# Two buffers of normed rows before the expert blocks, the second block's rows turned later, and the tenth expert matrix loaded after the token table

## The chip, the cores and the metric

The kernel runs on one core of a Trainium2 chip. The metric is device time in microseconds (us) of one execution; lower is better. TensorE is called PE, VectorE DVE, ScalarE ACT, GpSimd POOL and SyncE SP. SP and POOL mostly issue DMAs here.

## The reference, cut to what matters

One layer of a hybrid encoder on 512 prompt frames and 32 sample frames (544 tokens, width 1024): a token mixer (attention and a gated delta net, joined by an output projection) and then a mixture of 32 experts. Everything is in float32. The part that this change touches is the join of the two:

```python
x1 = x + einsum('btd,de->bte', gate_a * branch_a + gate_b * branch_b, w_out)
n = rmsnorm(x1, g_ffn)
grp_logits = n @ w_grp + b_grp           # 4 groups: pick the best
e_logits   = n @ w_exp + b_exp           # 32 experts: the best 2 inside that group
# each expert e, for the tokens that chose it:
h = silu(n[tok] @ w_e1[e]) * (n[tok] @ w_e3[e])
y[tok] += (h @ w_e2[e]) * weight
```

Each expert has three matrices of 2 MB (w_e1 and w_e3 1024x512, w_e2 512x1024); all 32 experts are read, 96 matrices in all.

## The kernel before, in words

The last part of the kernel is written in two functions whose engine programs run one behind the other on each engine: `project_and_choose`, then `expert_blocks`. The order of the work is written out by hand, and semaphores join the engines.

`project_and_choose` goes through five tiles of token rows (four of 128 prompt rows, i = 0 to 3, then the 32 sample rows, i = 4). For each tile PE finishes the second half of the output projection (L2084, counted in `projected`), DVE adds it to the residual rows (L2435), ACT forms the sum of squares and its root (L2287, L2288), DVE the reciprocal (L2439, `inverted`). PE turns the rows (L2313), ACT moves them out of the bank to `xT` (L2268), PE multiplies them with the router's weights (L2324), and DVE picks group and experts (L2442 to L2460) and counts ranks (L2420, L2424).

Beside it each tile's rows are written to a table in DRAM, `token_rows`, from which the expert blocks later gather. ACT scales the rows into one buffer `c_xn` (L2296) and POOL issues the DMA of 512 KB to the table (L2256). As there is one buffer, ACT waits ahead of L2296 until the table write of the tile before has landed (`tabled`, the wait at L2293). Everything that stands behind on ACT waits too: the move of the next tile's turned rows (L2268) first. The sample rows have two buffers of their own (L2300, L2259, `last_tabled`).

SP issues the expert matrices, each a DMA of 2 MB on one queue, in the order w_e1, w_e3, w_e2 of experts 0, 1 and 2, then w_e1 and w_e3 of expert 3 (eleven matrices, of which the tenth is w_e1 of expert 3, in buffer `e_w1_3`). The first six have no wait. The seventh waits for `projected` 2, the eighth for `projected` 4, the ninth and the tenth for `projected` 5, the eleventh (buffer `e_w3_3`, in which many small tiles of this function lie) for `normed` 5 and `picked`, the list of slots that DVE makes last (L2476).

`expert_blocks` runs 32 blocks, one for each expert (64 slots each), and further ones where an expert has more tokens. The first block's rows are picked on PE (L2350). Of the others POOL gathers the rows from the table (L2751 for blocks 1 and 2 once `last_tabled` is complete, L2541 later). A block on PE: up products with w_e1 and w_e3 (L2593, 64 matmuls), then the rows of the next block are turned (`ahead`, L2562 to L2566), then the hidden rows are turned (L2602), then the down product (L2611, 16 matmuls). Each buffer of weights is loaded again once its product is over: there are four for w_e1 and w_e3 and three for w_e2, and for the first of the reloads (L2183) w_e1 and w_e3 go in halves. Behind the last block the results, scattered to DRAM by choice, are read back and added (`y_rows`).

Of the kernel before, what the change touches and what calls it, by code (L numbers as in the profile page):

```python
# [19 lines left out]
ACT = mybir.ActivationFunctionType  # L20
AX = mybir.AxisListType

D = 1024
KD = D // 128
# [2079 lines left out]
ROW0 = [NP] + [128 * t for t in range(4)]  # L2104
# [63 lines left out]
def load_weights(k, sp, name, tiles, loaded, e, slot):  # L2168

    src = expert_matrix(k, name, e).rearrange("(p k) n -> p (k n)", p=128)  # L2170
    sp.dma_start(tiles[slot][:].rearrange("p k n -> p (k n)"), src).then_inc(loaded[slot], 16)  # L2171
# [20 lines left out]
def load_down(k, sp, e, slot):  # L2192

    src = expert_matrix(k, "w_e2", e).rearrange("(a p b) n -> p a (b n)", a=2, p=128)
    sp.dma_start(k.w2[slot][:].rearrange("p (a b) n -> p a (b n)", a=2), src).then_inc(k.w2_loaded[slot], 16)


def project_and_choose(k):
# [3 lines left out]

    nc, o = k.nc, k.out_stream
    V, T = nc.vector, k.early
    xn, xn_s, junk, xT = k.xn, k.xn_s, k.xn_s[1], [T(f"xT{m}", 4, 128) for m in range(3)]
    s0, s1, rt, rr = T("sum0", 5), T("sum1", 5), T("root", 5), T("rms", 5)
    iN, sN, token_i = T("iota_i", NE, dt=I32), T("slot_i", 2 * SLOTS, dt=I32), T("token_i", 5, dt=I32)
    gi, gf, pen, em, ei, ef = T("gidx", 8, dt=U32), T("gsel", 1), T("penalty", GROUPS), T("em", NE), T("eidx", 8, dt=U32), T("esel", 2)
    both, run, tmp = T("both", 3, NE), T("run", 2, NE), T("tmp", NE)
    r1, b1 = [T(f"rank_oh{j}", 2 * SLOTS) for j in range(2)], T("blk_oh", 2, NE)  # L2210
    made, padded, zeroed, based, weighed, added0, added1, squared, rms, tabled, turned, moved, scored, biased, chosen, \
        counted, ranked, listed, projected, columns, inverted, k.picked, k.normed = (k.sem("c_" + n) for n in (
            "made", "padded", "zeroed", "based", "weighed", "added0", "added1", "squared", "rms", "tabled", "turned", "moved",
            "scored", "biased", "chosen", "counted", "ranked", "listed", "projected", "columns", "inverted", "picked", "normed"))
    sums = both[:, 0:2, :].rearrange("p a e -> p (a e)")
    other, scaled = T("first_other", SLOTS), T("first_scaled", 1)
    k.tabled, placed = tabled, k.sem("c_placed")
    P, TA, TB, L, C, S = k.bank[0:2], k.bank[2], k.bank[3], k.bank[4:6], k.bank[6], k.bank[7]
    slot = lambda i: i % 2 if i < 4 else 2
    tiles = [(i, t, TILES[t][0], TILES[t][1]) for i, t in enumerate(ORDER)]  # L2220
    def on_sync(sp):
        for j in (2 * KD - 2, 2 * KD - 1):
            o.load(sp, j)
        sp.wait_ge(padded, 2)
        load_router(k, sp)
        for e in range(2):
            load_up(k, sp, e, e)
            load_down(k, sp, e, e)
        sp.wait_ge(projected, 2)
        load_weights(k, sp, "w_e1", k.w1, k.w1_loaded, 2, 2)  # L2230
        sp.wait_ge(projected, 4)
        load_weights(k, sp, "w_e3", k.w3, k.w3_loaded, 2, 2)
        sp.wait_ge(projected, 5)
        load_down(k, sp, 2, 2)
        load_weights(k, sp, "w_e1", k.w1, k.w1_loaded, 3, 3)
        sp.wait_ge(k.normed, 5)
        sp.wait_ge(k.picked, 1)
        load_weights(k, sp, "w_e3", k.w3, k.w3_loaded, 3, 3)

    def on_gpsimd(g):  # L2240
        g.memset(k.wr[:], 0.0).then_inc(padded, 1)
        g.memset(k.br[:], NEG).then_inc(padded, 1)
        g.iota(iN[:], pattern=[[1, NE]], base=0, channel_multiplier=0).then_inc(made, 1)

        g.iota(sN[:].rearrange("p (a g r) -> p a g r", a=2, r=SPREAD), pattern=[[0, 2], [1, SLOTS // SPREAD], [SLOTS // SPREAD, SPREAD]],
               base=0, channel_multiplier=0).then_inc(made, 1)

        g.iota(token_i[:], pattern=[[256, 5]], base=-256 - 2 * NT, channel_multiplier=2).then_inc(made, 1)
        g.wait_ge(made, 3)
        g.iota(token_i[:, 0:1], pattern=[[0, 1]], base=2 * NP - 2 * NT, channel_multiplier=2).then_inc(made, 1)  # L2250
        for j in (2 * KD - 2, 2 * KD - 1):
            o.split_lo(g, j)
        for i, t, c0, n in tiles:
            g.wait_ge(k.normed, i + 1)
            if i < 4:
                g.dma_start(k.table[ROW0[t]:ROW0[t] + n, :], xn[0:n, :]).then_inc(tabled, 16)  # L2256
            else:
                for h in range(2):
                    g.dma_start(k.table[ROW0[t]:ROW0[t] + n, 512 * h:512 * h + 512], xn_s[h][0:n, :]).then_inc(k.last_tabled, 16)  # L2259
        g.wait_ge(tabled, 64)  # L2260

    def on_scalar(a):
        def move(i, n, h, bank):
            m = 2 * i + h
            a.wait_ge(turned, m + 1)
            if m >= 3:
                a.wait_ge(scored, m - 2)
            nc.scalar.activation(xT[m % 3][:, :, 0:n], bank[:, 0:4 * n].rearrange("p (k n) -> p k n", k=4), ACT.Copy)\  # L2268
                .then_inc(moved, 1)

        c = k.chain(a, "scalar")
        for j in (2 * KD - 2, 2 * KD - 1):
            o.split_hi(a, j)
        a.wait_ge(zeroed, 1)
        for i, t, c0, n in tiles:
            a.wait_ge(added0, i + 1)
            nc.scalar.activation(junk[0:n, :], k.x[0:n, t, 0:512], ACT.Square, accum_out=s0[0:n, t:t + 1]).then_inc(squared, 1)
            a.wait_ge(squared, i + 1)
        move(0, tiles[0][3], 0, TA)
        for s in range(1, RING):  # L2280
            nc.scalar.activation(k.xg[:, s, :], k.striu[:, 0:1].broadcast_to([128, D // 2]), ACT.Copy).then_inc(k.cleared, 1)
        a.wait_ge(based, 1)
        for i, t, c0, n in tiles:
            if i >= 1:
                move(i, n, 0, TA)
            a.wait_ge(added1, i + 1)
            c(nc.scalar.activation(junk[0:n, :], k.x[0:n, t, 512:], ACT.Square, accum_out=s1[0:n, t:t + 1]))  # L2287
            nc.scalar.activation(rt[0:n, t:t + 1], s1[0:n, t:t + 1], ACT.Sqrt, bias=s0[0:n, t:t + 1],  # L2288
                                 scale=1.0 / D).then_inc(rms, 1)
            move(i, n, 1, TB)  # L2290
            a.wait_ge(inverted, i + 1)
            if 1 <= i < 4:
                a.wait_ge(tabled, 16 * i)  # L2293
            rows = k.x[0:n, t, :].rearrange("n (p k) -> n p k", k=KD)
            if i < 4:
                nc.scalar.activation(xn[0:n, :].rearrange("n (k p) -> n p k", k=KD), rows, ACT.Copy,  # L2296
                                     scale=rr[0:n, t:t + 1]).then_inc(k.normed, 1)
            else:
                for h in range(2):
                    last = nc.scalar.activation(xn_s[h][0:n, :].rearrange("n (k p) -> n p k", k=4), rows[:, :, 4 * h:4 * h + 4],  # L2300
                                                ACT.Copy, scale=rr[0:n, t:t + 1])
                last.then_inc(k.normed, 1)
# [179 lines left out]
def expert_blocks(k):  # L2482
# [4 lines left out]
    nc = k.nc  # L2487
# [8 lines left out]
    xT, hm, hT = k.xT, k.hm, k.hT  # L2496
    y = k.over("b_y", [128, D // 2], F32, "late", 16 * KD * FE)
    T = lambda name, *dims: k.sb("m_" + name, [128] + list(dims), F32, ctx)
# [19 lines left out]
    turned, copied = k.turned, k.copied  # L2518
# [140 lines left out]
    def places(b):  # L2659

        up_at = (b, 0) if b <= RING else ((b - 1) % RING, (b - 1) // RING)
        return up_at + (b % RING, b // RING, b % RING, b // RING - (b % RING == 0))

    def run_blocks(eng, part, beside=lambda s: None):

        for b in range(EARLY):
            part(eng, b, *places(b), False, places(b + 1)[4:])
            beside(b)
        eng.wait_ge(planned, 1)
        n = eng.value_load(k.nmore[0:1, 0:1], min_val=0, max_val=MORE)  # L2670
        with eng.Fori(EARLY // RING, LAST // RING - 1) as i:
            for s in range(RING):
                d2, past_d2 = (s + 1) % RING, (s + 1) // RING
                after = (s + 2) % RING
                part(eng, RING * i + s + 1, s, i, d2, i + past_d2, d2, i + past_d2 - (d2 == 0), False,
                     (after, i + (s + 2) // RING - (after == 0)))
        for b in range(LAST - RING + 1, NE - 1):
            part(eng, b, *places(b), False, places(b + 1)[4:] if b < LAST else None)
            beside(b)
        u, nu, d2, nd, half, m = places(LAST)  # L2680
        with eng.If(n > 0):
            with eng.Fori(0, n) as j:
                part(eng, j + NE - 1, u, j + nu + 1, d2, j + nd + 1, half, j + m + 1, True)
        part(eng, n + NE - 1, *places(NE - 1), True, halves=True)
        return n
# [159 lines left out]
    def on_vector(v):  # L2845
# [88 lines left out]
        c(V.tensor_copy(which[:], S[:, 0:2 * NE]))  # L2934
        c(V.tensor_tensor(which[:], which[:], S[:, 2 * NE:4 * NE], ALU.add))
        aim(which, NE, k.dst[:, 0:NE]).then_inc(targets, 1)
        v.wait_ge(k.tabled, 64)
        run_blocks(v, vector_part, beside)
        def add_choice(m, j, before):
            t = ORDER[m]  # L2940
# [87 lines left out]
```

## Time and profile before

| | |
|---|---|
| median of 3 runs | 1210.57 us (1208.8 to 1213.7) |
| time of the profiled execution | 1210.81 us |
| its span | 1209.1 us |
| PE busy | 1083.7 us (90%) |
| DVE, ACT, POOL busy | 36%, 29%, 32% |
| DMA over the span | 284.52 MB, mean 235 GB/s |
| mean granted clock of TensorE | 0.974 |
| largest share of the chain that ended last | 20%, DMA of expert weights |

The span is what the trace covers, 1.7 us less than the execution's own time. The granted clock is a share of 2.4 GHz: 1.00 is that level, 0.50 is 1.2 GHz. A DMA share is the mean busy share of the core's 16 DMA engines, and a share slightly above 1 is a full one. All times inside the trace are counted from the start of the span.

### The profile page before, as it was taken

The numbers are of one execution on the slowest core, as the hardware profiler recorded it, in microseconds if no ns is written. First come the engines' busy times: TensorE is split into PE (matmuls) and PEld (weight loads), VectorE is DVE, ScalarE is ACT, GpSimd is POOL, SyncE is SP. The second block draws the span as 40 slices with busy tenths as digits, with TensorE's granted clock in tenths as the row PEclk, the third lists the DMA queues.
The fourth block names the chain that finished last, engine by engine and source line by source line (L and its number), as shares of the span: only waits on it lengthen the run. The fifth ranks groups of instructions, "written<-read, shape, count | busy, mean of one in ns | idle before, by whom it ended". The sixth has DMA issues, their size and how long they took to land. (4 is left out here: it accounts for less than half of the span.)

```text
span 1209.1 us, 20612 instructions
## 1 busy us (share of the span) xinstructions
PE 1083.7 (90%) x8278; PEld 833.0 (69%) x8278; DVE 434.3 (36%) x995; ACT 355.1 (29%) x752; POOL 388.2 (32%) x426
## 2 busy tenths in 40 slices
PE   5999899899999989999999988999998777777777
PEld 4998888799999877888899764555554444444443
DVE  6598733793111264432242453222111111111115
ACT  5547633452222644453333422000000000000000
POOL 3554359843211443232464201212212111111100
PEclk9999989998988989999999988999999999999999
DMA  6422225345332621112531598999999999999998
GB/s 131 88 70 71 71 66 160 88 131 146 89 91 58 203 102 53 53 41 82 188 96 53 201 428 348 419 424 427 426 427 429 428 428 428 427 428 429 428 423 332
DMA packets 149677, 284.52 MB, mean 235 GB/s; under 512 B 43636, under 2 KB 118996, under 8 KB 132704
## 3 DMA queue, kind: packets, MB, share of 16 engines
q1 hardware_dynamic: 94288, 244.94, 52.0%
q10 hardware_dynamic: 49632, 27.46, 8.1%
q0 software_dynamic: 5680, 11.05, 2.4%
q8 instruction: 54, 0.88, 0.3%
q14 instruction: 23, 0.19, 0.0%
HBM read 266.81 MB, written 24.31 MB: 241 GB/s over the span
## 5 line engine op out<-in xcount | busy, mean ns | idle before, releaser
L2593 PE MATMUL bank<-e_w,b_xT 128*64 128x256 f32 x2048 | 231.3, 381 | 42.4 <-DMA e_w<-in_w_e 40.1
L499 PE MATMUL bank<-xhi,cv_w_hi 128*128 128x272 f32 x848 | 258.8, 305 | 8.6 <-PEq L145 2.6
L485 POOL TENSOR_TENSOR cv_w_lo<-cv_w_raw,cv_w_hi 128x1024 fp32r<-128x1024 f32 (+1 forms) x69 | 165.7, 2402 | 311.8 <-ACT cv_w_hi L478 311.4
L499 PE MATMUL bank<-xhi,cv_w_lo 128*128 128x272 f32 x848 | 249.5, 294 | 0.0
L499 PE MATMUL bank<-xlo,cv_w_hi 128*128 128x272 f32 x848 | 248.9, 294 | 0.0
L2593 PEld LDWEIGHTS bank<-e_w,b_xT 128*64 128x64 f32 x2048 | 149.1, 137 | 133.1 <-DMA e_w<-in_w_e 36.3
L499 PEld LDWEIGHTS bank<-xhi,cv_w_hi 128*128 128x128 f32 x848 | 164.4, 194 | 17.3 <-issue 9.7
L499 PEld LDWEIGHTS bank<-xlo,cv_w_hi 128*128 128x128 f32 x848 | 164.8, 194 | 1.0
L499 PEld LDWEIGHTS bank<-xhi,cv_w_lo 128*128 128x128 f32 x848 | 164.2, 194 | 0.0
L2638 DVE TENSOR_TENSOR b_hidden<-b_hidden,bank 128x256 f32<-128x256 f32 x32 | 13.5, 421 | 364.4 <-PE bank L2593 364.4
L2611 PE MATMUL bank<-e_w,b_hiddenT 128*64 128x512 f32 x512 | 116.9, 598 | 22.3 <-DVE b_hiddenT L2643 22.3
L2621 ACT ACTIVATE b_y<-bank 128x512 f32<-128x512 f32 x32 | 19.1, 597 | 299.2 <-PE bank L2611 299.2
L2550 POOL COPY b_target<-slot_target 128x1 int32 (+1 forms) x31 | 5.5, 177 | 312.3 <-ACT b_y L2621 280.2
L2611 PEld LDWEIGHTS bank<-e_w,b_hiddenT 128*64 128x64 f32 x512 | 37.2, 136 | 80.0 <-issue 52.0
L478 ACT ACTIVATE cv_w_hi<-cv_w_raw 128x1024 fp32r<-128x1024 f32 (+1 forms) x69 | 69.3, 1004 | 27.7 <-DMA cv_w_raw<-in_w_br_a 15.8
L687 DVE SCALAR_TENSOR_TENSOR conv_acc<-conv_in,wconv,conv_acc 128x547 f32<-128x547 f32 x48 | 60.5, 1260 | 1.7
L2618 ACT ACTIVATE b_hidden<-bank 128x256 f32<-128x256 f32 x32 | 12.3, 383 | 115.8 <-PE bank L2593 115.8
L2084 PE MATMUL bank<-o_hi,mix_prompt 128*128 128x512 f32 x128 | 43.2, 397 | 1.4 <-PEq L145 0.7
L499 PE MATMUL bank<-yb_hi,cv_w_hi 128*128 128x272 f32 x128 | 41.5, 324 | 1.4 <-DVE yb_lo L1657 1.4
L499 PE MATMUL bank<-yb_lo,cv_w_hi 128*128 128x272 f32 x128 | 38.4, 300 | 0.0
L499 PE MATMUL bank<-yb_hi,cv_w_lo 128*128 128x272 f32 x128 | 38.3, 299 | 0.0
L1926 ACT ACTIVATE f_probs<-f_probs,f_stat 32x160 f32<-32x160 f32 (+4 forms) x40 | 21.1, 528 | 54.8 <-DVE f_stat L1873 54.7
(449 smaller groups left out, 1660.4 us busy)
## 6 DMA issues: line engine op xcount, KB each, us to landing
e_w<-in_w_e SPq DMA_DIRECT2D x91, 2048.0 KB, 37.4
cv_w_raw<-in_w_in ACTq DMA_DIRECT2D x34, 512.0 KB, 3.9
e_w<-in_w_e SPq DMA_DIRECT2D x10, 1024.0 KB, 33.3
cv_w_raw<-in_w_in SPq DMA_DIRECT2D x18, 512.0 KB, 3.7
cv_w_raw<-in_w_br_b ACTq DMA_DIRECT2D x8, 512.0 KB, 4.0
o_raw<-in_w_out SPq DMA_DIRECT2D x16, 256.0 KB, 3.7
y_rows<-choice_rows SPq DMA_DIRECT2D x8, 512.0 KB, 7.0
g_values_gates<-g_z_stage ACTq DMA_DIRECT2D x12, 272.0 KB, 4.3
```

Of the source, the lines that this page charges most:

```text
L478: self.k.nc.scalar.activation(self.whi[:, c % OPS, 0:nk, :], self.raw[:, c % RAWS, 0:nk, :], ACT.Copy)\
L485: self.k.nc.gpsimd.tensor_tensor(self.wlo[:, s, 0:nk, :], self.raw[:, s, 0:nk, :], self.whi[:, c % OPS, 0:nk, :].bitcast(F32), ALU.subtract)\
L499: last = self.k.nc.tensor.matmul(self.bank(c, h)[:, 0:HALF], w, x[:, d, cols], start=(d == 0 and n == 0), stop=(d == nk - 1 and n == 2))
L687: op = nc.vector.scalar_tensor_tensor(out=ac[:, 0:W], in0=ci[:, w:w + W], scalar=k.wconv[:, w, c:c + 1], in1=ac[:, 0:W], op0=ALU.mult, op1 ...
L1926: last = nc.scalar.activation(pr[0:n, j % 2, x, 0:nk], pr[0:n, j % 2, x, 0:nk], ACT.Exp, bias=st[0:n, 1, 2 * j + x:2 * j + x + 1], accum_o ...
L2084: last = k.nc.tensor.matmul(bank[0:n, :], rows, w[:, d, :], start=(start and i == 0), stop=(d == KD - 1 and i == 2))
L2550: nc.gpsimd.tensor_copy(to[:], k.dst[:, bass.ds(column, 1)]).then_inc(aimed, 1)
L2593: last = nc.tensor.matmul(k.bank[bank][sl[a], 0:FH], xT[:, d, :], w[u][:, d, FH * a:FH * a + FH], start=(d == 0), stop=(d == KD - 1))
L2611: last = nc.tensor.matmul(k.bank[4][sl[a], :], hT[:, f % 2, sl[f // 2]], k.w2[d2][:, f, 512 * a:512 * a + 512], start=(f == 0), stop=(f == ...
L2618: nc.scalar.activation(hm[:], k.bank[1][:, 0:FH], ACT.Silu).then_inc(silu, 1)
L2621: nc.scalar.activation(y[:], k.bank[4][:], ACT.Copy).then_inc(out, 1)
L2638: nc.vector.tensor_tensor(hm[:], hm[:], k.bank[2][:, 0:FH], ALU.mult).then_inc(hidden, 1)
```

## The change

The normed rows get a second buffer, `xn_odd`, which lies among the small tiles in `e_w3_3`; tiles 0 and 2 use the old one, tiles 1 and 3 the new one. Each buffer has its own semaphore `tabled[j]`. ACT's wait ahead of L2296 now stands for tiles 2 and 3 alone, for the table write of two tiles before. On SP the tenth matrix is issued behind two waits, for `normed` 5 and for `last_tabled` 32, so once the sample rows' table writes have landed; the eleventh also waits for the second buffer's two table writes. In the expert blocks, block 0 no longer turns block 1's rows between its up and down products; block 1 turns them itself at its beginning, behind block 0's down product (`own` is true for b == 1).

```diff
-    xn, xn_s, junk, xT = k.xn, k.xn_s, k.xn_s[1], [T(f"xT{m}", 4, 128) for m in range(3)]
+    xn, xn_s, junk, xT = [k.xn, T("xn_odd", D)], k.xn_s, k.xn_s[1], [T(f"xT{m}", 4, 128) for m in range(3)]
...
-    k.tabled, placed = tabled, k.sem("c_placed")
+    k.tabled = tabled = [k.sem(f"c_tabled{j}") for j in range(2)]
+    placed = k.sem("c_placed")
...
         sp.wait_ge(projected, 5)
         load_down(k, sp, 2, 2)
+        sp.wait_ge(k.normed, 5)
+        sp.wait_ge(k.last_tabled, 32)
         load_weights(k, sp, "w_e1", k.w1, k.w1_loaded, 3, 3)
-        sp.wait_ge(k.normed, 5)
         sp.wait_ge(k.picked, 1)
+        sp.wait_ge(tabled[1], 32)
         load_weights(k, sp, "w_e3", k.w3, k.w3_loaded, 3, 3)
...
             if i < 4:
-                g.dma_start(k.table[ROW0[t]:ROW0[t] + n, :], xn[0:n, :]).then_inc(tabled, 16)
+                g.dma_start(k.table[ROW0[t]:ROW0[t] + n, :], xn[i % 2][0:n, :]).then_inc(tabled[i % 2], 16)
...
-        g.wait_ge(tabled, 64)
+        for j in range(2):
+            g.wait_ge(tabled[j], 32)
...
-            if 1 <= i < 4:
-                a.wait_ge(tabled, 16 * i)
+            if 2 <= i < 4:
+                a.wait_ge(tabled[i % 2], 16)
             rows = k.x[0:n, t, :].rearrange("n (p k) -> n p k", k=KD)
             if i < 4:
-                nc.scalar.activation(xn[0:n, :].rearrange("n (k p) -> n p k", k=KD), rows, ACT.Copy,
+                nc.scalar.activation(xn[i % 2][0:n, :].rearrange("n (k p) -> n p k", k=KD), rows, ACT.Copy,
                                      scale=rr[0:n, t:t + 1]).then_inc(k.normed, 1)
...
         for b in range(EARLY):
-            part(eng, b, *places(b), False, places(b + 1)[4:])
+            part(eng, b, *places(b), b == 1, places(b + 1)[4:] if b else None)
             beside(b)
...
-        v.wait_ge(k.tabled, 64)
+        for j in range(2):
+            v.wait_ge(k.tabled[j], 32)
```

## Rows read from the trace of the kernel before

**Rows 1.** The page's slices of the span in 40 parts: DMA busy share and rate.

```profile
DMA  6422225345332621112531598999999999999998
GB/s 131 88 70 71 71 66 160 88 131 146 89 91 58 203 102 53 53 41 82 188 96 53 201 428 348 419 424 427 426 427 429 428 428 428 427 428 429 428 423 332
```

**Rows 2.** Busy time by stretch: length, PE, PEld, DVE, ACT, POOL, clock, DMA share, GB/s.

```profile
683.00:725.00 42.00, 39.05 (x216) 31.07 (x215) 20.64 (x109) 16.36 (x26) 1.91 (x3) 0.92 1.01 422
725.00:728.00 3.00, 0.00 (x0) 0.00 (x0) 1.34 (x9) 1.83 (x2) 0.00 (x0) 0.69 0.77 303
728.00:738.00 10.00, 9.29 (x46) 4.70 (x46) 4.72 (x29) 3.46 (x8) 1.56 (x3) 0.58 1.02 390
738.00:743.00 5.00, 4.24 (x54) 2.61 (x54) 2.69 (x11) 0.73 (x1) 1.13 (x1) 1.00 0.46 127
743.00:760.00 17.00, 15.22 (x129) 8.84 (x127) 3.67 (x14) 3.52 (x7) 5.04 (x10) 1.00 1.00 404
760.00:893.00 133.00, 125.40 (x977) 69.92 (x975) 26.68 (x78) 9.81 (x20) 29.43 (x62) 1.00 1.01 426
893.00:1169.00 276.00, 220.37 (x1676) 123.97 (x1672) 33.31 (x88) 18.62 (x38) 50.57 (x108) 1.00 1.01 428
```

**Rows 3.** The chain that ended last, in order of time: start, length, what.

```profile
689.57 10.77 DMA token_rows<-c_xn
...
714.77 11.31 DMA token_rows<-c_xn
...
732.77 7.93 DMA token_rows<-c_xn_sample
...
741.61 8.49 DMA b_rows<-token_rows,slot_token
...
897.34 35.60 DMA e_w<-in_w_e
```

**Rows 4.** Timeline of ACT, 700 to 730: start, length, line, idle before and its releaser.

```profile
704.64 0.60 ACT L2268 ACTIVATE c_xT<-bank 128x512 f32<-128x512 f32 x1 [0.70 <-PE bank L2313]
712.44 2.04 ACT L2296 ACTIVATE c_xn<-x_rows,c_rms 128x1024 f32<-128x1024 f32 x1 [7.21 <-DMA token_rows<-c_xn]
...
714.28 0.62 ACT L2268 ACTIVATE c_xT<-bank 128x512 f32<-128x512 f32 x1
...
726.17 2.02 ACT L2296 ACTIVATE c_xn<-x_rows,c_rms 128x1024 f32<-128x1024 f32 x1 [8.56 <-DMA token_rows<-c_xn]
```

**Rows 5.** Timeline of PE, 706 to 751.

```profile
706.20 0.48 PE L2084 MATMUL bank<-o_hi,mix_prompt 128*128 128x512 f32 x1
...
714.96 1.12 PE L2324 MATMUL bank<-c_w_router,c_xT 128*128 128x40 f32 x8 [2.20 <-ACT c_xT L2268]
...
719.38 0.63 PE L2084 MATMUL bank<-o_hi,mix_sample 128*32 128x512 f32 x1
...
728.35 0.74 PE L2324 MATMUL bank<-c_w_router,c_xT 128*32 128x40 f32 x8 [3.57 <-ACT c_xT L2268]
...
741.75 7.13 PE L2593 MATMUL bank<-e_w,b_xT 128*64 128x256 f32 x64 [0.53 <-DVE b_xT L2629]
750.14 0.32 PE L2562 MATMUL bank<-ident,b_rows 64*128 64x64 f32 x1 [1.26 <-DMA b_rows<-token_rows,slot_token]
```

**Rows 6.** SP's queue, the issues of weights from 709 to 749.

```profile
709.22 0.33 SPq L2171 DMA_DIRECT2D e_w<-in_w_e  x1
723.88 0.38 SPq L2195 DMA_DIRECT2D e_w<-in_w_e  x1
...
740.53 0.33 SPq L2171 DMA_DIRECT2D e_w<-in_w_e  x1
743.74 5.51 SPq L2183 DMA_DIRECT2D e_w<-in_w_e  x4
```

**Rows 7.** The table writes of the four prompt tiles (L2256), issue to landing.

```profile
DMA to landing us min/median/max: 9.5/11.0/11.9
```

**Rows 8.** The page's DMA issues: count, KB each, median us from issue to landing.

```profile
out_y_p<-x_rows SPq DMA_DIRECT2D x4, 512.0 KB, 3.3
```

More of the change, by code:

```diff
@@ L2210, in project_and_choose @@
     r1, b1 = [T(f"rank_oh{j}", 2 * SLOTS) for j in range(2)], T("blk_oh", 2, NE)
-    made, padded, zeroed, based, weighed, added0, added1, squared, rms, tabled, turned, moved, scored, biased, chosen, \
+    made, padded, zeroed, based, weighed, added0, added1, squared, rms, turned, moved, scored, biased, chosen, \
         counted, ranked, listed, projected, columns, inverted, k.picked, k.normed = (k.sem("c_" + n) for n in (
-            "made", "padded", "zeroed", "based", "weighed", "added0", "added1", "squared", "rms", "tabled", "turned", "moved",
+            "made", "padded", "zeroed", "based", "weighed", "added0", "added1", "squared", "rms", "turned", "moved",
             "scored", "biased", "chosen", "counted", "ranked", "listed", "projected", "columns", "inverted", "picked", "normed"))
```

## The prediction

> **What bounds the kernel now.** I read the page's slices first [rows 1]: up to slice 22 the DMA engines are half idle, and from slice 23 (about 695 us) to the end they are full, at 419 to 429 GB/s but for slice 24 with 348. That is the reading of expert weights, and slice 24 (725 to 756 us) is where this change works. Then the stretches [rows 2]. From 743 us to 1169 us, 426 us long, the DMA share is 1.00 to 1.01 at 404 to 428 GB/s. PE is busy 94% of 760 to 893 and only 80% of 893 to 1169 (220.37 of 276). Third the chain of waits [rows 3]. Before 742 us it runs over ACT's normed rows and the table writes (10.77, 11.31 and 7.93 us stand in the rows, a fourth of 9.47 us lies between, 39 us in sum), then over a gather and PE's blocks, and from 897 us on it is made of hops on the weights, 35.6 us and longer. The chain would have one gain from everything that goes off the first part. But PE's early lead is given back: whatever PE gains before 893 it waits for afterwards, because the weights' stream through the DMA engines is full from 743 us on. So the question is when that stream could have been at the same place, that is, how much time the DMA engines idle between 683 and 743 us, and not when PE starts its blocks.
>
> That idle time, length times one less the share [rows 2]: 725 to 728, 3 x 0.23 = 0.7 us; 738 to 743, 5 x 0.54 = 2.7 us. Together 3.4 us. The rate is also lower where table writes are mixed in: 728 to 738 at 390 instead of 428 GB/s is 10 x 38/428 = 0.9 us, 743 to 760 at 404 is 1.0 us, 683 to 725 at 422 is 0.6 us. Even all of it recovered makes 5.9 us, 0.5% of the time; nothing here can give more unless the reason above is wrong.
>
> **The change part by part.**
>
> *ACT's wait for the table.* It removes waits of 4.8 us (tile 1, not in the rows), 7.21 us and 8.56 us ahead of L2296 [rows 4]. Tile 1's hides behind PE: PE's later chunk of projection starts at 706.20 after a gap of 0.3 us or so in either case, so I count nothing. For tile 2 ACT is free at 705.24 [rows 4] and the first table write landed at 700.34 [rows 3], so the normed rows are made from 705.3 to 707.3. The turned rows of tile 3, which ACT moved at 714.28 only because it stood in that wait [rows 4], are moved as soon as PE has turned them, and PE doesn't idle the 2.20 us before 714.96 [rows 5]. Its router product starts at about 712.7. From there to the next chunk of projection it took 4.42 us (714.96 to 719.38), in the preceding tile about 3.15 us at clock 1.00; the chunk itself took 719.38 to 723.88 [rows 5, 6], 4.5 us, against 706.20 to 709.22, 3.0 us. The clock between was 0.50 for most of that (mean 0.92 over 683 to 725 [rows 2]), that is the 1.2 GHz level, and it fell just behind the idle 2.20 us. I take it that it doesn't fall: `projected` 5 comes at 712.7 + 3.15 + 2.9 = 718.8 instead of 723.9. If it falls all the same, 712.7 + 4.4 + 4.5 = 721.6. For tile 3 the wait goes too (the second write lands near 709). The 3.57 us of idle PE before 728.35 [rows 5] go with it; the router product of the sample rows starts at about 720, 8 us earlier, and the sample's normed rows, made at 729.9 to 732.0 before, at about 721.5 to 723.5. Late next is DVE's choice, about 3 us a tile, and PE's first rows. From the sample's router product to the first block it was 728.35 to 741.75, 13.4 us, at mean clock 0.58 over most of it; at clock 1.00 some 2 us less. So block 0 starts at 720 + 11.5 = 731.5 with the clock up, and at about 735 with it down: 7 to 10 us earlier.
>
> *The table.* The five tiles' writes are issued at 689.6, 698, 707.5, 717.3 and 723.5/724. Under the full stream they took 9.5 to 11.9 us each [rows 7], the sample's 7.93 us [rows 3]. Two of them are now under way at once for the first time, so nothing in this trace prices that. From below: no dearer, the last lands at 724.0 + 7.9 = 731.9. From above: strictly one behind the other, 689.6 + 10.8 + 9.5 + 11.3 + 11.9 + 7.9 = 741. I take 732, since before too the queue of weights beside each write was full, and 512 KB in 11 us is a ninth of the rate, which leaves room for a second.
>
> *The tenth matrix behind the table.* The ninth is issued at `projected` 5, at 719 (721.6 at worst). The eighth, issued at 709.22 [rows 6], ran the engines dry only at 725, so the dip of 0.7 us is gone. Without the tenth the engines run dry at 738.7 (where the share falls in 738 to 743) less one matrix, 2.1 MB at 428 GB/s = 4.9 us, less the 0.7: at 733.1. The tenth is issued at the landing, 732, and its first bytes come 0.7 us behind (the eleventh, issued at 740.53 [rows 6], had the engines busy again at about 741.2): 732.7. That is a hair ahead of the dry point, but the landing of a write comes after its last byte, and each start of the queue before had a ramp of about half a us. I take a gap of 0.8 us; bounds nothing (landing at 731 or earlier) and 8.6 us (landing at 741). The eleventh waits for `picked`, 10 us earlier like block 0, so at 731 to 734, and the tenth covers until 738. The reloads (L2183) start at 733 to 737 instead of 743.74, with two matrices, 9.8 us, queued ahead of them. No further gap.
>
> *The Trainium skill against this step.* Before, the engines ran dry at about 738.7 and the gathers behind `last_tabled` were issued at 741.61 [rows 3], some 2 us behind the last byte. "DMA: Bandwidth & Descriptors", section "Anatomy of one DMA", gives about 2 us of fixed cost, most of it the receipt of the write, heaviest for HBM. By it a load that waits for a table write can't follow on without a gap: if the table is the last in the queue the gap is about 2 us and 0.7 us for the start, and the gain 0.7 us instead of 2.6 us. The trace agrees with the size; whether the table is last here it doesn't tell. Both results lie in the range.
>
> *The second block's rows.* In block 0 PE's wait of 1.26 us for the gather goes [rows 5], and the turn, 0.6 us, moves. In block 1 the turn and DVE's two scaled copies of 0.42 us stand alone: +1.5 us of PE. The gather, 8.49 us [rows 3], lands at about 741, ahead of block 0's end at 731.5 + 12.4 = 744. PE net -1.3 to +1.8 us; on the end nothing, as PE's lead of several us over the stream up to 893 hides it. Were this cover gone it would cost +0.2 us.
>
> *Semaphores and the second buffer.* Two waits on POOL and DVE in place of one, a few tens of ns each, off the path: nothing. The buffer's overlap with `e_w3_3` only matters by the added wait, met by then (731.9).
>
> **The sum.** Gap before 3.4 us, gap after 0.8 us: -2.6 us, against the profiled execution 1210.81 - 2.6 = 1208.2. That execution lies 0.2 us above the median of the runs (1210.57), so the median becomes 1208.0; with the rate beside the table unchanged I leave 1208.2.
>
> **The rivals.**
>
> A. *The gap stays.* The table's landing or the clock takes away what the earlier projection brings: landing at 734.5, gap 734.5 + 0.7 - 733.1 plus a ramp of 0.5 = 2.6 us, or the tenth matrix's new wait leaves the engines as idle as before. Gain 0 to 0.8 us, time 1210.3. For it: the receipt; that the tenth is queued later relative to the table than it was. Against: the 5 us by which the projection ends earlier.
>
> B. *PE's start sets the end.* Block 0 starts 7 to 10 us earlier and the end follows: 1210.6 - 8.5 = 1202. For it: the chain of waits runs over PE until 893. Against: DMA share 1.01 over 133 us of it, and PE's idle 20% behind it [rows 2]. I can think of no way but a rate above 428 GB/s.
>
> C. *Slower: the writes hold each other up.* Place: the sample rows' table write. If two writes in flight share one write's pace, the last lands at up to 741; the tenth matrix, the eleventh and all reloads stand behind it on SP, and the engines are dry from 733.1 to 741.7, 8.6 us against 3.4: +5.2 us, 1215.8. It costs from a landing at 735.5 on. For it: the 11 us under load. Against: with the weights gone the writes have the engines alone, and 512 KB out of SBUF took 3.3 us outside this full stream [rows 8]. So the likelier size is a landing at 735 to 736, and the 741 an end.
>
> D. *The change doesn't do what it says*: PE or DVE is late where ACT was, and `projected` 5 comes at 723 anyway. Then the tenth matrix issues 8 us later than before (at the old landing, 740.8), the engines are dry from 733.8 to 741.5, and the time is 1210.6 + 5 = 1215.5. Against: each of the waits on ACT is put down to the table's write.
>
> **How the numbers follow.** The forecast (gap of 0 to 2 us, 1206.8 to 1209.5) has 0.60, A 0.20, C 0.08, D 0.05, B 0.07. The predicted time is the forecast's, 1208.2. Runs of before spread by 5 us, so a median can be off by 1.5 us. The range 1204.8 to 1212.0 holds the forecast and A with that spread (0.8 less the spread's tails, and the milder part of C); outside lie B, D and most of C. What a measurement of this kernel can tell from no change is about 0.5%, 6 us: faster means below 1204.5, which is B and a tail, 0.09; slower means above 1216.6, which only the ends of C and D with the spread reach, 0.06; same 0.85.
>
> **What would show it.** In the trace after: no idle ahead of L2296 for tile 1, and little for 2 and 3; PE's 2.20 and 3.57 us gone; clock 1.00 from 716 to 723 (else the second value holds); ninth matrix issued near 719; sample's table landed at 732, tenth issued behind it at once; DMA share in a stretch around 733 with a single dip of under 1.5 us; block 0 at 731 to 735; PE waiting for weights already from about 860 instead of 893; and from 745 on the same 424 to 428 GB/s. The forecast is wrong if the stream after the dip is not full, if the landing comes after 735, or if the end moves by more than the idle DMA time does.

## The result

The changed kernel took 1204.83 us (median of 12 runs), the kernel before 1211.72 us: ratio 0.9947, 95% interval 0.9924 to 0.997, that is 0.3 to 0.8% faster and 6.4 us by the ratio. One of the 12 runs of the kernel before took 4914 us and can't belong to this ratio; without it the median is 1210.57 us. Another 12 runs of the changed kernel (e5 below) gave a median of 1207.89 us and a ratio of 0.9959 (0.9938 to 0.998). The forecast, 1208.2 us and so 2.6 us less, had the direction and the place right and about half the size. The time lies 0.03 us above the lower end of the stated range, 1204.8. That it lies inside is luck, as the median of the same kernel differs by 3 us between the two sets of runs; it is also only 0.3 us short of the 1204.5 from which the forecast would have called it faster, with a chance of 0.09.

The page of the changed kernel has the DMA engines full from slice 23 on. Slice 24, with 348 GB/s before [rows 1], has 422:

```profile
DMA  6422225445332531112632499999999999999998
GB/s 132 89 71 71 71 66 158 91 117 147 97 97 57 184 123 54 50 40 67 201 92 67 167 423 422 427 427 425 425 428 429 427 428 428 428 428 429 429 422 323
```

The same stretches as in [rows 2], of the changed kernel (columns as there: length, PE, PEld, DVE, ACT, POOL, clock, DMA share, GB/s):

```profile
683.00:725.00 42.00, 40.48 (x248) 31.11 (x246) 24.59 (x133) 22.53 (x34) 3.48 (x6) 0.96 1.01 423
725.00:728.00 3.00, 3.00 (x18) 1.11 (x16) 1.56 (x10) 0.00 (x0) 0.00 (x0) 0.96 0.95 401
728.00:738.00 10.00, 9.24 (x102) 6.03 (x102) 2.98 (x12) 3.27 (x5) 3.59 (x5) 1.00 1.02 429
738.00:743.00 5.00, 3.86 (x22) 1.48 (x20) 2.64 (x10) 0.00 (x0) 0.00 (x0) 1.00 0.99 416
743.00:760.00 17.00, 15.86 (x132) 8.91 (x130) 4.40 (x18) 1.58 (x3) 3.96 (x9) 1.00 1.02 424
760.00:893.00 133.00, 125.33 (x987) 70.53 (x985) 24.65 (x66) 10.22 (x21) 30.93 (x65) 1.00 1.01 427
893.00:1169.00 276.00, 216.19 (x1631) 121.29 (x1629) 32.55 (x86) 17.70 (x36) 47.91 (x102) 1.00 1.01 427
```

The two dry places, shares 0.77 and 0.46 [rows 2], are 0.95 and 0.99 now: of 3.4 us idle DMA time, counted by the share, 0.2 us is left. The rates beside them went up too, from 390 to 429 and from 404 to 424 GB/s.

ACT, start and length, with the idle time before and its releaser; to be read against [rows 4]:

```profile
704.98 2.10 ACT L2300 ACTIVATE c_xn<-x_rows,c_rms 128x1024 f32<-128x1024 f32 x1
709.54 0.60 ACT L2272 ACTIVATE c_xT<-bank 128x512 f32<-128x512 f32 x1 [2.46 <-PE bank L2317]
...
714.51 2.10 ACT L2300 ACTIVATE c_xn_odd<-x_rows,c_rms 128x1024 f32<-128x1024 f32 x1
...
721.51 2.14 ACT L2304 ACTIVATE c_xn_sample<-x_rows,c_rms 32x512 f32<-32x512 f32 x2 [0.67 <-DVE c_rms L2443]
```

No copy of normed rows waits for a table write; ACT now waits for PE and DVE. PE, against [rows 5]:

```profile
714.67 1.08 PE L2328 MATMUL bank<-c_w_router,c_xT 128*128 128x40 f32 x8 [0.32 <-ACT c_xT L2272]
715.59 0.41 PE L2084 MATMUL bank<-o_hi,mix_sample 128*32 128x512 f32 x1
...
719.38 0.47 PE L2328 MATMUL bank<-c_w_router,c_xT 128*32 128x40 f32 x8
...
731.49 7.13 PE L2597 MATMUL bank<-e_w,b_xT 128*64 128x256 f32 x64 [0.53 <-DVE b_xT L2633]
...
743.84 0.32 PE L2566 MATMUL bank<-ident,b_rows 64*128 64x64 f32 x1
...
745.04 7.13 PE L2597 MATMUL bank<-e_w,b_xT 128*64 128x256 f32 x64 [0.58 <-DVE b_xT L2633]
```

The idle 2.20 and 3.57 us are gone and block 0 starts at 731.49 instead of 741.75. SP's issues of weights, against [rows 6]:

```profile
718.56 0.38 SPq L2195 DMA_DIRECT2D e_w<-in_w_e  x1
729.69 1.08 SPq L2171 DMA_DIRECT2D e_w<-in_w_e  x2
733.48 5.51 SPq L2183 DMA_DIRECT2D e_w<-in_w_e  x4
```

The ninth matrix goes out 5.3 us earlier, the tenth and the eleventh together once the table is complete. The sample rows' two table writes, issued from 723.94 on, took 5 us each to land (the first line; in the kernel before, the chain has 7.93 us [rows 3]), the prompt tiles' 9.4 to 10.8 us (the second line), no more than before [rows 7]. They hardly overlap: they are issued at 689.67, 698.31, 707.37 and 716.90, so each is at most 2 us on its way when the one before lands:

```profile
DMA to landing us min/median/max: 4.9/5.0/5.1
...
DMA to landing us min/median/max: 9.4/10.1/10.8
```

The chain of waits up to 887 us runs over PE, with pieces on DVE and ACT between and without a DMA, and then over the weights. The last line is a matrix from its issue to its landing; the one that stands in this place before was issued 10 us later [rows 3]:

```profile
721.93 3.53 PE bank L2354 x8
...
731.49 7.15 PE bank L2597 x64
...
883.67 3.48 PE bank L2597 x32
...
887.31 40.56 DMA e_w<-in_w_e
```

So PE's blocks start 10.3 us earlier and the span is 5.5 us shorter (1203.6 against 1209.1): about half of what PE gained is waited off later. PE's first wait for a matrix ends at 897.24 in the changed kernel (the first line) and at 922.65 before (the second), and from 760 to 1170 us PE waits 43.1 us for weights instead of 40.1:

```profile
897.24 3.67 PE L2597 MATMUL bank<-e_w,b_xT 128*64 128x256 f32 x32 [1.39 <-DMA e_w<-in_w_e]
...
922.65 3.67 PE L2593 MATMUL bank<-e_w,b_xT 128*64 128x256 f32 x32 [1.06 <-DMA e_w<-in_w_e]
```

### The profile page after: what moved, and what is told of

The parts are those of the page before. It is cut to its first block and busy times, and to the rows that moved or that the text cites. A ratio compares the mean times of both kernels' runs of the same rounds, so it can differ in the third digit from the quotient of the medians.

```text
span 1203.6 us, 20613 instructions
## 1 busy us (share of the span) xinstructions
PE 1076.3 (89%) x8278; PEld 826.9 (69%) x8278; DVE 432.1 (36%) x995; ACT 356.6 (30%) x752; POOL 389.3 (32%) x426
## 5 line engine op out<-in xcount | busy, mean ns | idle before, releaser
L2597 PE MATMUL bank<-e_w,b_xT 128*64 128x256 f32 x2048 | 231.6, 381 | 46.1 <-DMA e_w<-in_w_e 43.1
## 6 DMA issues: line engine op xcount, KB each, us to landing
e_w<-in_w_e SPq DMA_DIRECT2D x10, 1024.0 KB, 33.3
```

The source lines that it names most:

```text
L2597: last = nc.tensor.matmul(k.bank[bank][sl[a], 0:FH], xT[:, d, :], w[u][:, d, FH * a:FH * a + FH], start=(d == 0), stop=(d == KD - 1))
```

## The experiments

Eight kernels, one of them the changed kernel again, were timed with 12 runs each against the kernel before. A second measure comes from the trace. The first expert matrix is issued at 676.5 to 685.0 us in executions of kernels that are the same up to there (e8, where that issue was moved, aside). That spread is as large as the runs' own, so the table gives the time from that issue to the end of the span as well. The last two columns are the bytes moved in 80 us, from 1 us behind that issue on (five stretches of 45, 3, 10, 5 and 17 us, length times rate), and the rate in 743:760 or the stretch that answers to it.

| kernel | ratio to before (95%) | first issue to end | MB in 80 us | GB/s then |
|---|---|---|---|---|
| before | | 529.1 us | 30.8 | 404 |
| after | 0.9947 (0.9924 to 0.997) | 523.6 | 33.5 | 425 |
| e5 after again | 0.9959 (0.9938 to 0.998) | 523.4 | 33.5 | 426 |
| e1 two buffers | 0.9953 (0.9931 to 0.9975) | 523.7 | 33.4 | 424 |
| e4 buffers, turn | 0.9953 (0.993 to 0.9977) | 523.9 | 33.3 | 423 |
| e2 tenth only | 1.0009 (0.9988 to 1.0031) | 530.8 | 30.6 | 394 |
| e3 turn only | 1.0011 (0.9987 to 1.0035) | 530.2 | 30.6 | 399 |
| e6 tenth late | 1.0009 (0.9986 to 1.0031) | 528.4 | 31.1 | 419 |
| e7 PE late | 0.9965 (0.9941 to 0.9988) | 523.7 | 33.5 | 425 |
| e8 stream early | 0.9956 (0.9932 to 0.9979) | 524.4 | 33.0 | 423 |

**e1, two buffers alone.** The changed kernel with its other two parts put back:

```diff
         load_down(k, sp, 2, 2)
-        sp.wait_ge(k.normed, 5)
-        sp.wait_ge(k.last_tabled, 32)
         load_weights(k, sp, "w_e1", k.w1, k.w1_loaded, 3, 3)
+        sp.wait_ge(k.normed, 5)
         sp.wait_ge(k.picked, 1)
...
-            part(eng, b, *places(b), b == 1, places(b + 1)[4:] if b else None)
+            part(eng, b, *places(b), False, places(b + 1)[4:])
```

> The change without its other two parts: two buffers of normed rows alone; the tenth matrix issued with the ninth as before, the second block's rows turned inside block 0 as before. Theory S (the end moves by the time that the weights' DMA engines are not full between 681 and 760 us, and by nothing else): the tenth matrix is queued at about 719, the queue covers until 738, the eleventh comes with `picked` at 730.5, so there is no dry stretch: all of the whole change's gain, 5 to 6 us, DMA share 0.97 or more in 725:743. Rival T (the earlier landed token table, got by holding the tenth matrix back, carries part of it): a gain of 3 us or less, the sample's table write landing 8 us after its issue instead of 5.7, and PE waiting about 1 us in block 0 for the gather.

All of the gain is there: 523.7 us. The stretches behind the first issue (at 684.98) have no dry place (columns: length, granted clock, DMA share, GB/s):

```profile
685.95:730.95 45.00, 0.96 1.01 412
730.95:733.95 3.00, 1.00 0.97 410
733.95:743.95 10.00, 1.00 1.03 432
743.95:748.95 5.00, 0.85 0.99 417
748.95:765.95 17.00, 0.94 1.02 424
```

Rival T falls on the end: PE does wait 1.94 us for the gather in block 0, as it said, and that doesn't reach the end. Its other sign didn't come: the sample's two table writes, issued from 729.95 on, took 4.9 and 5.5 us, against 4.9 and 5.1 in the changed kernel, and not 8. The first gather is issued 7.05 us behind the first of them here and 7.28 us there.

**e4, the whole change without the tenth matrix's move.**

```diff
-        sp.wait_ge(k.normed, 5)
-        sp.wait_ge(k.last_tabled, 32)
         load_weights(k, sp, "w_e1", k.w1, k.w1_loaded, 3, 3)
+        sp.wait_ge(k.normed, 5)
```

> The whole change but for the tenth matrix, which is issued with the ninth as before. Theory S: same as the whole change, as neither has a dry stretch (5 to 6 us less than before). Rival T: 1 us or more slower than the whole change.

523.9 us, 0.3 us from the whole change and as near to e1: nothing that this measure can tell.

**e2, the tenth matrix's move alone,** on the kernel before:

```diff
+        sp.wait_ge(k.normed, 5)
+        sp.wait_ge(k.last_tabled, 32)
         load_weights(k, sp, "w_e1", k.w1, k.w1_loaded, 3, 3)
-        sp.wait_ge(k.normed, 5)
```

> The kernel before with the tenth matrix alone moved behind the landed token table. Theory S: the engines run dry at about 733 instead of 738.7; the sample's table write, issued at 732.3, then has them to itself and lands near 736; the tenth follows, then the eleventh at 740.5; the dry time is 3 to 4 us instead of 3.4: no change, -0.5 to +2 us. Rival T: faster by 2 us or more, since the gathers start some 5 us earlier. Rival Q (a matrix less of cover is a matrix lost): slower by 4.9 us.

No change in time, 1.7 us more in the trace, inside theory S's bounds and against both rivals. The dry place moved to earlier stretches (first issue at 680.51):

```profile
726.48:729.48 3.00, 0.93 0.92 276
729.48:739.48 10.00, 0.68 0.83 283
739.48:744.48 5.00, 1.00 0.97 374
744.48:761.48 17.00, 0.90 0.99 394
```

But theory S's measure, the time that the engines are not full, doesn't give these 1.7 us. By the share 2.3 us are idle here, against 2.8 us in the same stretches of the kernel before (3 x 0.05 + 10 x 0.04 + 5 x 0.44), so the end should have come a little earlier. The bytes have the right sign: 0.26 MB less in the 80 us, 0.6 us at 428 GB/s, and 424 instead of 426 GB/s over the next 133 us, another 0.6 us. The remaining 0.5 us stay open.

**e3, the second block's turn alone,** on the kernel before:

```diff
-            part(eng, b, *places(b), False, places(b + 1)[4:])
+            part(eng, b, *places(b), b == 1, places(b + 1)[4:] if b else None)
```

> The kernel before with the second block's rows turned behind block 0's down product and nothing else. Theory S: PE's blocks move by -1.3 to +1.8 us, the weights' stream doesn't: no change, within 0.5 us in the trace from 681 us on. Rival P (where PE's blocks stand sets the end, as the chain of waits has it until 893 us): the end moves with block 1, by -1.3 to +1.8 us.

No change in time, 1.1 us more in the trace, over the 0.5 us of theory S. In this execution the clock was 0.51 in the ten us ahead of block 0 and the stream was dry for longer (first issue at 682.23):

```profile
731.20:741.20 10.00, 0.51 0.80 333
741.20:746.20 5.00, 0.82 0.46 108
746.20:763.20 17.00, 0.95 0.99 399
```

That is 10 x 0.20 + 5 x 0.54 = 4.7 us idle, against 2.8 in the same stretches of the kernel before. In bytes it is 0.29 MB less, 0.7 us, and 425 instead of 426 GB/s over the next 133 us is another 0.3, together 1.0 of the 1.1 us. The edit acts only behind the up products of block 0, which begins at 744.45, when most of the dry time is over, so most of this difference can't come from the edit. Block 1 also began 2.2 us later, and this run alone doesn't separate the two. e7 does.

**e6, the tenth matrix held back.** In the changed kernel:

```diff
         sp.wait_ge(k.last_tabled, 32)
+        sp.wait_ge(k.begun, 2)
         load_weights(k, sp, "w_e1", k.w1, k.w1_loaded, 3, 3)
```

> The changed kernel with the tenth matrix held back on purpose, until block 0's product with w_e3 is half done (about 5.3 us into block 0). PE's blocks start as in the changed kernel. Theory S (dry time of the stream sets the end, one for one): nine matrices and the table run out at about 732, the tenth's first bytes come at 737.6: some 5.5 us dry, so 5 to 6.5 us more from the first issue to the end, about 529. Rival P (PE's blocks set the end while they are the chain): no change, 523.6, since block 3, the first to need the tenth, is 35 us away.

4.9 us more than the changed kernel's two executions (523.5 on average), and the gain is gone in the timed runs too (1.0009). PE's block 0 starts 51.2 us behind the first issue as before this edit (51.0 and 51.5), block 1 at 64.7 (64.6 and 65.0); only the stream is interrupted:

```profile
724.37:727.37 3.00, 1.00 0.96 403
727.37:737.37 10.00, 1.00 0.64 208
737.37:742.37 5.00, 1.00 0.96 405
742.37:759.37 17.00, 1.00 1.00 419
```

Idle are 3.9 us by the share. In bytes it is 2.4 MB less in the 80 us than in the changed kernel, 5.7 us at 428 GB/s, so the 4.9 us lie between the two measures, and just under theory S's 5 to 6.5. Rival P falls.

**e7, PE held back.** In the changed kernel, ahead of block 0, with six more matmuls in float32 into a bank that is written again:

```diff
         pe.wait_ge(k.joined, 1)
+        pe.wait_ge(k.w1_loaded[0], 16)
+        for d in range(6):
+            nc.tensor.matmul(k.bank[1][:], k.ident[:], k.w1[0][:, d, :], start=True, stop=True)
         turn_first().then_inc(turned, 1)
```

> The changed kernel with six more matmuls of 128x512 in float32 on PE ahead of block 0, into a bank that is written again later: by the rows of this kernel about 0.85 us each, 5.1 us. Theory S: no change from the first issue to the end (523.6 within 0.5 us), since the two matrices queued behind the table cover the later reloads and PE only waits less from 880 us on. Rival P: 5 us more.

The extra work took 5.42 us and block 0 started at 740.63 - 684.26 = 56.4 us behind the first issue, 4.9 and 5.4 us later than in the changed kernel's two executions:

```profile
733.23:743.23 10.00, 1.00 1.02 433
743.23:748.23 5.00, 1.00 0.98 412
748.23:765.23 17.00, 1.00 1.02 425
```

The stream went on full and the end came at 523.7 us; PE waited 39.3 us for weights from 760 to 1170 instead of 43.1. PE's place can move by 5 us without a trace at the end: this and e6 together show that the stream sets the end and PE's blocks don't.

**e8, the stream started earlier.** In the changed kernel the first matrix goes out behind three of the six router DMAs, and DVE waits for the other three later:

```diff
         load_router(k, sp)
-        for e in range(2):
-            load_up(k, sp, e, e)
-            load_down(k, sp, e, e)
+        load_weights(k, sp, "w_e1", k.w1, k.w1_loaded, 0, 0)
+        load_router(k, sp, True)
+        load_weights(k, sp, "w_e3", k.w3, k.w3_loaded, 0, 0)
+        load_down(k, sp, 0, 0)
+        load_up(k, sp, 1, 1)
+        load_down(k, sp, 1, 1)
```

> The changed kernel with the first expert matrix issued ahead of the last three of the six small router DMAs (the biases and the gain, which now have a semaphore of their own that DVE waits for at the first tile's logits). The first matrix is issued about 1.6 us earlier in the stage, and all behind it. Theory S: the end comes 1 to 1.6 us earlier, counted from the first router DMA; against the kernel before 7 us. Rival P: the same or later, since the biases land behind 2 MB and DVE can be late with the first tile by a few us, which moves PE's blocks later by as much.

Counted from the first router DMA it took 527.4 us, the changed kernel's two executions 527.8 and 527.9. A gain of 0.4 to 0.5 us instead of 1 to 1.6, so theory S's number missed, and in the timed runs none that can be told (0.9956 beside 0.9959). The first matrix went out 1.1 and 1.5 us earlier than in those two, but the second to the sixth 0.1 to 0.8 us later, as three small DMAs stood between, and the stream ran at 403 GB/s in its first 45 us instead of 415:

```profile
675.42:720.42 45.00, 0.96 0.99 403
```

No version of these is clearly better than the changed kernel.

**e5, the changed kernel again,** with no edit.

> The changed kernel once more, on the chip of the next three. From the issue of the first expert matrix to the end of the span it took 523.6 us, the kernel before 529.1; the part ahead of that issue has differed by 8.5 us between executions of programs that are alike there (676.5 to 685.0), so the span alone is a poor measure. Both theories: 523.6 within 0.5 us.

523.4 us: the measure repeats within 0.2 us where the times themselves spread by 8 us.

## Why the prediction was right in its reason and short in its size

**The bound.** Right. The end moves with the weights' stream and not with PE (e6, e7). Over all ten executions the bytes in the 80 us go with the end: from the kernel before to the changed one 2.6 MB more is 5.5 us less, where 2.6 MB at 428 GB/s would be 6.2 us.

**ACT's wait and PE's times.** Right: `projected` 5 at 718.8 forecast, the ninth matrix issued at 718.56; sample rows issued at 723.5/724, measured 723.94 and 0.5 us later. Block 0 at 731.5, measured 731.49, is in part luck: the sample rows' router product began at 719.38 instead of 720, and from there it took 12.1 us instead of 11.5. The granted clock, 0.50 behind the idle 2.20 us before, stayed at 1.00 from 716 to 721. It was 0.50, the 1.2 GHz level, from 722 to 725, behind an idle 0.68 us and a stretch of small router matmuls, in the first rows' products, which took 3.53 us for 8 matmuls where the next 12 took 2.90 us. By these two PE paid some 1.6 us for it, an estimate; e7 shows that the end paid nothing.

**The gap before.** The first term that was mis-sized: 3.4 us, counted as length times one less the DMA share. A share is time, and the stream is bytes. In 738 to 743 the share was 0.46 but the rate only 127 GB/s, 0.30 of the full 428. By the rate the two dry places [rows 2] are 3 x 125/428 = 0.9 and 5 x 301/428 = 3.5 us, 4.4 us in all, 1.0 us more than forecast. With it the bound for everything recovered is 6.9 us and not 5.9.

**The gap after.** The second: 0.8 us, with a landing at 732. The table had landed by 729.69, as the sample's writes took 5 us, not 7.9, and the engines were not dry by then. What is left is 0.2 us by the share and 0.3 us by the rate (3 x 27/428 + 5 x 12/428), 0.5 us of the miss. That "nothing in this trace prices" two writes at once was a misreading: before, tile 3's write (issued at 728.48, 11.9 us on its way) and the sample's (from 732.25 on, 7.2 and 7.9 us) were under way together for 8 us, and in the changed kernel they overlap by 3.4 us only.

The sentence from the Trainium skill, "DMA: Bandwidth & Descriptors", section "Anatomy of one DMA", with 0.7 us of gain, doesn't bite here, because the table write wasn't the last in the queue: when it had landed, the stream of weights was still full (share 1.00 and 422 GB/s in 729 to 731). In e2 it was the last: the tenth matrix could go out 3.4 us behind the issue of the sample's writes, with the engines running dry around it. In the kernel before, the landing itself, at 740.70, stands 2.0 us behind the forecast's last byte; the gather's issue, which the forecast took for it, stands 2.9 us behind.

**The rate beside the table.** The third, and the largest, was "with the rate beside the table unchanged": I had worked out 0.9 us for 728 to 738 and 1.0 us for 743 to 760, put them down to table writes mixed in, and left them out. They came back almost whole, (429 - 390) x 10 / 428 = 0.9 us and (424 - 404) x 17 / 428 = 0.8 us, 1.7 us in all. For 743 to 760 table writes can't be the cause, as the last had landed at 740.7; and in 683 to 725 the stream ran at 422 and 423 GB/s with table writes beside it most of the time. Nearly half of what is missing there stands in one place, 3 us behind the issue of a single matrix at 755.41. By then the queue was short: the 6.3 MB issued since 740.53 (a matrix and four halves), moving from 741 on at about 420 GB/s, are through at about 756, an estimate:

```profile
746.00:748.00 2.00, 1.00 0.90 377
...
756.00:758.00 2.00, 1.00 1.06 426
758.00:760.00 2.00, 1.00 0.95 332
```

2 x 96/428 = 0.4 us of the 0.95. In the changed kernel the matrix that answers to it is issued at 743.95, behind 8.4 MB issued since 729.69, and there is no such dip (428, 417 and 440 GB/s in 743 to 748, 748 to 757 and 757 to 760). That the short queue makes the dip is argued and not tested. All four executions with a dry place have a lower rate over the 17 us, 394 to 419 GB/s; the six without have 423 to 426. But e6, where the dry place was made by the edit, has 419, 0.2 us, so a dry place by itself explains little of the loss. Why 728 to 738 ran at 390 GB/s stays open: in the kernel before, two table writes and the restart fall together there, and no run parts them.

**The sum again.** The dry places by the rate, 4.4 - 0.3 = 4.1 us, and the two rates, 1.7 us, make 5.8 us, against 5.5 in the trace. The forecast's 2.6 us were short by 1.0 (share for rate), 0.5 (gap after) and 1.7 (rate beside).

**The tenth matrix and the turn.** Priced at nothing on the end, and nothing they are. The turn removed the wait of 1.26 us in block 0 and put 1.1 us between block 0's down product (to 743.9) and block 1 (745.04), so from block 0's start to block 1's it is 13.55 us instead of 13.45. The tenth matrix's move brings no earlier landing: the sample's writes took 4.9 to 5.1 us with it and 4.9 to 5.5 us without (e1, e4).

**PE waiting again.** Forecast from about 860 instead of 893; the first wait ended at 897.2 (1.39 us), and at 922.7 before (1.06 us). Both numbers of the forecast were too early; that PE would wait again, and earlier than before, was right. In trace time PE lost 10.3 - 5.5 = 4.8 us of its gain.

**The rivals.** A (gap stays) and C (writes hold each other up) fell with the landing, D with the ninth matrix at 718.56, B with e7. Two prices for D don't hold. The tenth was issued with the ninth before, at 724.3, so at 740.8 it would be 16.5 us late and not 8. And e2, which comes close to D (the new wait without the earlier projection), cost 1.7 us in the trace, not 5: with the weights running out the sample's writes took about 3 us, and the tenth went out at 735.75.

## What to carry to other kernels

Where a DMA stream is full to the end, price every edit ahead of it by the bytes that the stream is behind, not by idle share: here a share of 0.46 hid a rate of 0.30. A chain of waits that runs over an engine with a lead shows what moves that engine, not the end. A stretch of lower rate near a dry one is part of the sum, and a forecast that leaves it out needs a reason from the rows. And look at what a part of a change gives alone: here one extra buffer was all of it, and the two other parts had no price either way.

## What the runs showed of the hardware

A stream of 2 MB weight loads that had run dry moved 394 to 419 GB/s over the 17 us behind (share of the engines 0.99 to 1.00), against 423 to 426 GB/s (1.02) when it had not; where the dry place was made by the edit alone (e6) it was 419. Beside the full stream a table write of 512 KB on POOL's queue took 9.2 to 11.9 us. One of 64 KB took 4.9 to 5.5 us where the big one ahead of it landed within some 4 us, and 6.2 to 7.9 us where that was still under way for 7 to 8 us (before, e3); with the stream running out (e2) the two of them took about 3 us. A DMA share of 0.46 went with 127 GB/s, 0.30 of the full rate. And the part of the kernel before this stage took 676.5 to 685.0 us (to its first issue) in kernels that are the same there, while the stage behind it repeated within 0.5 us between like kernels: for a change inside one stage the trace's own interval is the finer measure.
